# Feed-forward of a two-layer encoder: two products per later group split, and joins, casts and loads reordered around the group borders

## The reference

```python
def _convffn(h, buf, w_up, conv_w, w_down):
    a = jnp.einsum('bld,df->blf', h, w_up)
    a, buf_new = _causal_dwconv(a, buf, conv_w)
    gate, up = jnp.split(a, 2, axis=-1)
    return jnp.einsum('blf,fd->bld', jax.nn.silu(gate) * up, w_down), buf_new
```

## Time and profile before

| | us |
|---|---|
| median of 3 runs | 3333.78 |
| lowest and highest | 3327.42, 3337.51 |
| the profiled execution, its own time | 3342.18 |
| its span | 3340.40 |
| TensorE busy in the span | 3110.3 (93%) |
| GpSimd, VectorE, ScalarE busy | 1608.3, 2161.8, 1278.7 |
| pairs 20 to 31 of layer 0, from 1387.2 to 1623.2 | 236.0 |

### The profile page before, as it was taken

The page is one execution under the profiler, slowest core; times in us unless marked ns, Lnnn a source line. Parts: engine busy times, 40 slices in busy tenths (PEclk is TensorE's granted clock), DMA queues, the critical chain, the costliest instruction groups (busy, mean ns, idle before and its releaser), DMA issues. The chain is left out here.

```text
span 3340.4 us, 60986 instructions
## 1 busy us (share of the span) xinstructions
PE 3110.3 (93%) x24826; PEld 2863.1 (86%) x24826; DVE 2161.8 (65%) x3139; ACT 1278.7 (38%) x2379; POOL 1608.3 (48%) x1198
## 2 busy tenths in 40 slices
PE   7999998899999999989989999979899999999997
PEld 5988875688999999988978889648799999998886
DVE  5396464564578777766666855545626887777566
ACT  4244144233434444433233431532434344443332
POOL 3222120214578888677443211102246798887663
PEclk9999998799999999999999999978999999999998
DMA  5733231202112222522255313330021222226222
GB/s 191 193 112 110 82 121 44 85 3 76 65 60 83 77 76 74 183 93 81 76 176 158 117 66 97 100 121 9 20 87 63 73 73 76 73 73 218 91 66 77
DMA packets 194974, 310.50 MB, mean 93 GB/s; under 512 B 38212, under 2 KB 125508, under 8 KB 191624
## 3 DMA queue, kind: packets, MB, share of 16 engines
q1 hardware_dynamic: 192616, 303.46, 27.8%
q10 hardware_dynamic: 2080, 3.15, 0.3%
HBM read 214.24 MB, written 89.82 MB: 91 GB/s over the span
## 5 line engine op out<-in xcount | busy, mean ns | idle before, releaser
L2592 PE MATMUL PS<-t_highs,block_high 128*128 128x288 f32 x1480 | 438.4, 296 | 24.0 <-ACT kept_sum_b L2831 12.2
L260 POOL TENSOR_TENSOR w_split<-w_full,w_split 128x1024 fp32r<-128x1024 f32 (+1 forms) x76 | 191.1, 2515 | 540.4 <-ACT w_split L252 540.4
L2596 PE MATMUL PS<-t_highs,block_low 128*128 128x288 f32 x1480 | 438.4, 296 | 0.0
L265 PE MATMUL PS<-h_split,w_split 128*128 128x384 f32 x1152 | 413.5, 359 | 22.7 <-PEq L198 11.9
L2594 PE MATMUL PS<-h_split,block_high 128*128 128x288 f32 x1452 | 429.7, 296 | 0.0
L267 PE MATMUL PS<-h_split,w_split 128*128 128x384 f32 x1152 | 393.6, 342 | 0.0
L266 PE MATMUL PS<-h_split,w_split 128*128 128x384 f32 x1152 | 392.9, 341 | 0.0
L2592 PE MATMUL PS<-h_split,block_high 128*128 128x288 f32 x1260 | 379.6, 301 | 0.2
L2596 PE MATMUL PS<-h_split,block_low 128*128 128x288 f32 x1260 | 371.5, 295 | 0.0
L2594 PE MATMUL PS<-x_lows,block_high 128*128 128x288 f32 x1120 | 330.0, 295 | 0.0
L2592 PEld LDWEIGHTS PS<-t_highs,block_high 128*128 128x128 f32 x1480 | 279.3, 189 | 27.4 <-issue 27.4
(11 more groups left out here) (521 smaller groups left out, 7909.1 us busy)
## 6 DMA issues: line engine op xcount, KB each, us to landing
raw<-in_w_up SPq DMA_DIRECT2D x120, 256.0 KB, 2.9
act_keep<-ffn_up SPq DMA_DIRECT2D x44, 576.0 KB, 2.8
w_full<-in_w_in SPq DMA_DIRECT2D x40, 512.0 KB, 3.5
kq_keep<-split_rows SPq DMA_DIRECT2D x128, 128.0 KB, 2.4
kq_row<-kq_keep SPq DMA_DIRECT2D x32, 512.0 KB, 4.2
x<-x_keep SPq DMA_DIRECT2D x2, 4608.0 KB, 16.9
x_keep<-x SPq DMA_DIRECT2D x16, 576.0 KB, 5.4
raw<-in_w_down SPq DMA_DIRECT2D x48, 192.0 KB, 3.0
```

The lines of the kernel that those rows point to most:

```text
L260: pool.tensor_tensor(ws[:, slot_of(n), 1, 0:w], wf[:, n % WSLOTS, 0:w], ws[:, slot_of(n), 0, 0:w].bitcast(F32), ALU.subtract).then_inc(w_l ...
L265: pe.matmul(out, w_hi, a_hi, start=first, stop=False)
L2592: pe.matmul(out[:, j], w_hi[i][:, w], moving(t, s, 0, k, cols), start=FRESH[i] and k == 0, stop=False, skip_group_check=True)
L2596: mm = pe.matmul(out[:, j], w_lo[i][:, w], moving(t, s, 0, k, cols), start=False, stop=k == inner(s) - 1, skip_group_check=True)
```

## The change

- `FIRST` and `SECOND`: in the first pair of groups 1 and 2 (pairs 24 and 28) S4/B22 and A12/B21 are split and no longer whole. Group 0 stays as it is. `last_whole` follows, and TensorE waits there for the parts (`rdy`).
- GpSimd gets a function `low_of_rows`: it makes B22's low part (before on VectorE, in pair 25) and B21's (before in its own program for pair 26) while TensorE is in the border pair or in pair 24, plus the low parts of the two weight blocks.
- ScalarE: in a border pair 23 or 27 all three copies out of PSUM stand ahead of the casts of B11, B22, B21; T3's cast moves to the first pair of the group, before the copy of `kept_sum_c`, T4's after the third copy.
- VectorE: `lower_right` comes ahead of T1's sum and low part, `upper_left` ahead of T2's; in pair 4 T4's low half moves behind `lower_right`; in pair 21 the last gating product moves behind it.
- SP: for g = 1 the two staged loads of 864 KB go one pair ahead, into pair 21, around the last store of `act_keep`; the other two stay in pair 22.

The diff, cut to its core:

```diff
@@ WHOLE @@
             SECOND = ((S4, S3, A12, A22),) + ((S3, A22),) * (GROUPS - 1)
+            FIRST = ((A11, S1, S2, S4, S3, A12, A22),) + ((A11, S1, S2, S3, A22),) * (GROUPS - 1)
             for g in range(GROUPS):
-                WHOLE[UPS + HK * g] = (A11, S1, S2, S4, S3, A12, A22)
+                WHOLE[UPS + HK * g] = FIRST[g]
                 WHOLE[UPS + HK * g + 1] = SECOND[g]
 
             def last_whole(g, i):
-                return UPS + HK * g + (1 if i in SECOND[g] else 0)
+                return UPS + HK * g + (1 if i in SECOND[g] else 0 if i in FIRST[g] else -1)
@@ SP @@
                         if s == UPS + 1:
+                            sp.wait_ge(cvd, 2 * FF_TILES)
+                            sp.wait_ge(kst, 2 * FF_TILES)
+                            load_staged_12(1)
                             store_act(FF_TILES - 1)
-                            sp.wait_ge(kst, 2 * FF_TILES)
+                            load_staged_22(1)
                             sp.dma_start(d["o_fconv"][l], new[:, :, :]).then_inc(sout, 16)
                         if s == UPS + 2:
                             sp.wait_ge(aout, 16 * FF_TILES)
-                            load_staged(1)
+                            load_staged_21(1)
@@ TensorE @@
-                                elif (s - UPS) % HK in (1, 2):
+                                elif (s - UPS) % HK < HK - 1:
                                     pe.wait_ge(rdy[t], (s - UPS) // HK + (3 if t < B11 else 1))
@@ GpSimd @@
+                    def low_of_rows(b, g):
+                        i = MOVING.index(b)
+                        pool.wait_ge(chi[b], g + 1)
+                        pool.wait_ge(pdn, 7 * last_whole(g, i) + i + 1)
+                        for k in range(GK):
...
+                            ins = pool.tensor_tensor(b_rows(h2, 1, b)[:, k], raw, b_rows(h2, 0, b)[:, k].bitcast(F32),
+                                                     ALU.subtract)
+                        ins.then_inc(rdy[b], 1)
...
                         sum_of(s, S4)
+                        if first is not None and first >= 1:
+                            low_of_rows(B22, first)
                         low_of(s, S2)
                         sum_of(s, S3)
                         low_of(s, S4)
                         low_of(s, S3)
+                        if first is not None and first >= 1:
+                            low_of_rows(B21, first)
                         low_of(s, A12)
@@ ScalarE @@
                         keep_sum(s, 0)
+                        if after is not None and after >= 1:
+                            cast_sum(T3, after)
...
-                        elif after is not None:
-                            cast_sum(T4, after)
-                        if behind and s < UPS:
-                            high_of(n, S1)
-                        if border is not None and border >= 1:
-                            cast_rows(B11, border)
                         keep_sum(s, 2)
                         if s == UPS + 1:
                             gate(FF_TILES - 1)
-                        if behind and s >= UPS:
+                        if border is not None and border >= 1:
+                            cast_rows(B11, border)
+                            cast_rows(B22, border)
+                            high_of(n, S4)
+                            cast_rows(B21, border)
+                            high_of(n, A12)
+                        if behind:
                             high_of(n, S1)
+                        if after is not None and after >= 1:
+                            cast_sum(T4, after)
@@ VectorE @@
                     for s in range(UPS - 1):
                         f = s + PLAIN
                         upper_right(s)
-                        if s == 4:
-                            low_of_sum(T4, 3)
                         lower_right(s)
                         if s < 3:
                             low_of_sum((T1, T2, T3)[s], s)
+                        elif s == 4:
+                            low_of_sum(T4, 3)
                         upper_left(s)
...
                         upper_right(s)
+                        lower_right(s)
                         if s == UPS + 1:
                             product(FF_TILES - 1)
+                        if g is not None:
+                            t1_sum(g)
                         if step == 0:
                             low_of_sum(T1, s)
+                        upper_left(s)
                         if g is not None:
                             t2_sum(g)
-                        lower_right(s)
                         if step == 0:
                             low_of_sum(T2, s)
-                        if s == last_whole((s - UPS) // HK, S4):
-                            low_of_rows((s - UPS) // HK)
+                        if s == last_whole(0, S4):
+                            low_of_rows(0)
```

52 lines of the change are left out of this document (22 added, 30 removed).

## The result

| | before | changed |
|---|---|---|
| median | 3330.6 (4 runs) | 3362.81 (4 runs) |
| lowest, highest | 3327.08, 3337.51 | 3353.88, 3364.82 |
| ratio, 95% interval | | 1.0071 [1.0047, 1.0096] |
| the profiled execution: own time, span | 3342.18, 3340.40 | 3353.88, 3352.1 |

What follows compares the result with a forecast made beforehand. TensorE, busy 93% of the span, was taken as the bound. Terms summed to -3.5 us per layer, -7.0 for both, from 3342.2 to 3335.2; the shown median being 8.4 lower gave 3326.8 us, range 3312 to 3338.

Steps and rivals of the forecast that it cites:

- Pairs 3 to 5: Pair 4 on VectorE: T4's low half behind the join makes product 7 late; +2.0 us per layer, bounds 0 to +3.3.
- Pairs 20 to 23: Pair 20's gain is lost, staged loads delay raw_11 in pair 22, pair 23's wait goes; net +2.5 us per layer.
- Rival one: Pair 22: staged loads do not delay raw_11; 5.5 to 7 us less per layer, 3314 us; chance 0.19.
- Pair 27: Pair 27: ScalarE's copy goes ahead of the B11 cast; -1.0 us per layer.
- Pairs 24, 25, 28, 29: First two pairs of groups 1 and 2: split products, joins ahead of low parts, and what is late next; -7.0 us per layer.
- The split products' -2.0: Pairs 24 and 28: two products split in each, four at 0.50 us saved; -2.0 us per layer.
- The joins' -3.0 and -3.6: VectorE's joins ahead of low parts: pair 24's wait goes, -1.5 twice, and pair 25's, -1.8 twice, per layer.
- what is late next: Pairs 24 and 25: later sums T1 to T4, T3's cast and T2's low part; +0.8 us per group, +1.6 per layer.
- rival three: Pair 24: stalls only move, T1 to T4 sums and T3's cast cost 1.5 us more per group; 3333 us; chance 0.12.
- rival two: Pair 25: GpSimd becomes the bound, product 1 waits for B11's low part; +5.5 us per group, 3349 us; chance 0.12.
- The price of GpSimd's six new pieces: Pair 24 on GpSimd: three pieces for B22 and three for B21, taken at 1.6 to 2 us each.
- where the queue ends: GpSimd ends B11's low part some 19 us after pair 24 begins, pair 25 begins at 19.4 or later; cost nothing.

Runs made afterwards that it cites:

- e10: e9 with SP's load of raw_12 for pair 21 ahead of x, and pair 20's joins ahead of the low parts; ratio to the kernel before 0.9921.
- e11: The changed kernel with split products and GpSimd's pieces kept, plus the edits of e1, e4, e5, e6 and e10's on SP; ratio to the kernel before 0.9975.
- e6: The changed kernel with SP's two staged loads of 864 KB back in pair 22, behind raw_11; ratio to the kernel before 1.0025.
- e9: e8 with B22's cast behind pair 24's first copy, and T3's, B21's, T4's casts and S1's high part behind third copies; ratio to the kernel before 0.9925.
- e3: The changed kernel with GpSimd making only the last of three pieces of B22's and of B21's low part; ratio to the kernel before 1.0014.
- e1: The changed kernel with ScalarE's three copies out of PSUM ahead of T2's and T3's casts in pairs 24 and 28; ratio to the kernel before 1.0048.
- e4: The changed kernel with T1's sum before the join of kept_sum_b and T2's right after that of kept_sum_c in border pairs; ratio to the kernel before 1.0042.
- e2: The changed kernel with VectorE's sums of T1, T2 and T3 ahead of the joins again in border pairs; ratio to the kernel before 1.0038.
- e8: The kernel before with e7's copy order and VectorE's joins ahead of T1's and T2's sums and low parts; ratio to the kernel before 0.9966.
- e5: The changed kernel with pair 4's VectorE order undone, T4's low half ahead of the join of kept_sum_c; ratio to the kernel before 1.0046.
- e7: The kernel before with ScalarE's copy of kept_sum_b ahead of B11's cast in border pairs; ratio to the kernel before 1.0004.

## Why the prediction was wrong

By its own steps, per layer:

- *Pairs 3 to 5*, +2.0: measured +1.5. Product 7 of pair 4 waited 3.1 us as written and the slow stretch came (1.6); the waits of pair 3 (0.8) and pair 5 (1.45) went too, the first of which I had not counted. Pair 4 by itself cost 3.8, so the close sum is in part luck.
- *Pairs 20 to 23*, +2.5: measured +2.5 (+3.5 and +1.5). Pair 20's gain died in pair 21, and it lives once raw_12 goes ahead of x (e10, e11). The staged loads held raw_11 up by 5.2 us, where bytes over the busiest row's rate gave 5.4; product 4 of pair 22 came 6.7 and 5.9 us later, 5.8 as forecast; pair 23's wait went. Rival one is out (e6).
- *Pair 27*, -1.0: -1.2.
- *Pairs 24, 25, 28, 29*, -2.0 - 3.0 - 3.6 + 1.6 = -7.0: measured **+5.1**. This is the whole miss: 12.1 us per layer, 24 in all. The split products' -2.0 held (2.1). The joins' -3.0 and -3.6 are there once nothing else is late: -3.5 and -2.6 in e9.

The step that failed is the term "what is late next", +0.8 per group with bounds 0 to 3. It measured 6.9 by the prediction's own prices: 4.7 of wait and 1.4 of slow stretch in pair 24 (25.5 less 19.4 us), and 0.9 in pair 25 (18.8 less 17.9). I had seen each of its parts, the sums behind the joins, a cast ahead of a copy, new work on GpSimd, and named rival three and rival two for them. What I got wrong is the price of VectorE's sums. I took it from rows of the kernel before in which GpSimd idled, 1.35 and 0.75 us, and showed none of them, though the earlier trace rows spread from 1398 to 2505 ns for one shape and the earlier trace rows had 2.55 us for 1,152 columns at a time when GpSimd was at work. Here one shape with two durations was the mark of a neighbour. With four of the six pieces gone (e3) the term measures 2.8 (21.1 less 19.4, 19.0 less 17.9), which is inside its bounds, though not 0.8.

The price of GpSimd's six new pieces was about right: 4.73 us for B22's and 6.3 for B21's, where 1.6 to 2 us each gave 9.6 to 12. But B21's had a nearer row than B11's, their own in the kernel before (in GpSimd's program for pair 25; "for pair 26" above is wrong), and two of its three took 2.5 us each:

```profile
1495.89 5.01 POOL L2759 TENSOR_TENSOR h_split<-ffn_up,h_split 128x576 fp32r<-128x576 f32 x2
1500.86 1.42 POOL L2759 TENSOR_TENSOR h_split<-ffn_old,h_split 128x576 fp32r<-128x576 f32 x1
```

What did not hold is where the queue ends: some 19 us after pair 24 begins by the prediction, 23.5 in the changed kernel and 26.4 in e11.

The two rivals that the text held apart are one mechanism, and they cover each other. The stall in pair 24 gave GpSimd the time to finish B11's low part; e1, e4 and e11, which kept the pieces and took that stall away in part or whole, moved it to the start of pair 25, and e2 moved it into the border pair. I gave them 0.12 each and added their prices to the rest of the sum as if only one could be.

For this the Trainium skill has a rule that I did not weigh ("SBUF — State Buffer", Who interferes with whom): a VectorE instruction with two inputs in SBUF contends with a GpSimd instruction that reads SBUF, and the contention is an exclusive lock on the ports that the two share. The traces agree that they contend. Subtractions of two SBUF tiles of 128x1152 take 1.34 us alone and 2.56 to 2.59 beside GpSimd, the additions to x 0.76 (e8) and up to 1.99, while the join of kept_sum_a with a PSUM bank takes 0.74 either way, in the very middle of the busy stretch (1473.55 above). Not every overlap costs: in e4 an addition to x took 0.76 us in the middle of B22's pieces. What no run here shows is the lock itself; a queue for one port would look like this.

Shown by runs: that at these orders the pieces make 4.4 us of a group's stall (e3), that GpSimd becomes the bound behind it (e1, e4, e11), the staged loads (e6), pair 4 (e5), and that the gain of the joins and copies is there once GpSimd is left alone (e9). Open: the 8 us between the stages of the traces (16) and the ratio of the changed kernel (24), 16 by the medians.

## What to carry to other kernels

Price an operation by a row in which its neighbours are as busy as they will be after the change; where one shape has two durations, find out which engine runs beside the long one before moving more work to it. Count moved work twice, once on the engine that gets it and once on VectorE if both read SBUF. When several waits lie behind one another, taking one away prices the next (e1, e4, e7, e8). With GpSimd left as it was the orders paid 0.34% while product 3 of pairs 24 and 28 still waited (e8) and 0.75% without that wait (e9); with the added pieces the best of them paid 0.25% (e11).

## What the runs showed of the hardware that I had not expected

- The slowing is mutual: VectorE 128x1152 from 1.34 to 2.59 us (1.9 times), 128x576 from 0.74 to 1.97 (2.7 times); GpSimd 128x384 from 1.00 to 1.52 or 2.11, and three pieces of 128x576 in a row between 4.64 and 6.29.
- Neither the length of a wait nor its place alone tells whether the clock falls behind it. In e1, pair 24 of layer 0 waited 2.3 us with no slow stretch and pair 28 waited 2.3 us with one that cost 1.7 us. Waits of 4.5 us and more had it every time in these pairs, e3's of 1.8 us before product 3 never; in e6 one of 3.3 us had it (pair 24 of layer 1) and one of the same length had not (layer 0).
